# Branch products of two transformer layers: four-byte products replaced by three rounded products, with their high and low parts made beside the gates

## The reference, cut to what matters

```
gates = jax.nn.sigmoid(gate_logit)                 # u @ w_in, 4 * 1024 columns
branches = (y_pool, y_conv, y_moba, y_fox)
for n in range(N_BRANCH):
    term = gates[..., n * D_MODEL:(n + 1) * D_MODEL] * (branches[n] @ w_branch[n])
    merged = term if merged is None else merged + term
mixed = merged @ w_o
```

## Time and profile before

| | |
|---|---|
| median of 3 runs | 1328.84 us (1328.0 to 1331.78) |
| the profiled execution | 1324.11 us, of which the span is 1322.3 us |
| TensorE matmul busy | 1276.3 us, 97% of the span |
| VectorE busy | 933.9 us, 71% |
| ScalarE busy | 522.5 us, 40% |
| mean granted clock of TensorE | 0.996 |

### The profile page before, as it was taken

One profiled execution on the slowest core, in us unless ns is written; L12 is line 12 of the kernel. 1 busy time (PEld: TensorE's weight loads), 2 busy tenths in 40 slices (PEclk: granted clock), 3 DMA queues, 4 the chain that ended last, 5 costly groups with the idle time before them and its releaser, 6 DMA issues.

```text
span 1322.3 us, 18840 instructions
## 1 busy us (share of the span) xinstructions
PE 1276.3 (97%) x7793; PEld 1059.0 (80%) x7793; DVE 933.9 (71%) x1239; ACT 522.5 (40%) x805; POOL 107.9 (8%) x152
## 2 busy tenths in 40 slices
PE   5999999999999999999999999999999999999996
PEld 2798756448965479889988898987998998899895
DVE  5867687658768665777898666676587789654557
ACT  3322146214346043553344434334354434443432
POOL 2201110100000110011002000001011100000000
PEclk9999999999999999999999999999999999999999
DMA  9743550416620584677973776536567794355551
GB/s 372 243 139 106 180 188 1 150 45 237 206 80 1 187 273 155 241 281 272 314 276 131 252 250 249 191 128 255 187 238 264 276 332 170 127 190 182 184 185 56
DMA packets 104910, 257.75 MB, mean 195 GB/s; under 512 B 8213, under 2 KB 11766, under 8 KB 104570
## 3 DMA queue, kind: packets, MB, share of 16 engines
q1 hardware_dynamic: 80872, 172.40, 38.1%
q0 software_dynamic: 20192, 75.58, 15.9%
q10 hardware_dynamic: 3762, 8.57, 1.8%
HBM read 255.49 MB, written 1.05 MB: 194 GB/s over the span
## 4 chain that ended last, share of the span: by engine, by line
PE 82%; DVE 9%; ACT 4%; DMA 2%; issue 2%; POOL 1%; POOLq 0%; ACTq 0%; DVEq 0%
PE bank L823 80%; PE bank L990 3%; DVE weights_low L2327 1%; DMA start_ring<-in_w_mod_dram 1%; ACT odd_prob L1919 1%; DVE negated_maxima L2572 1%; DVE modulation_sums L2182 1%; ACT weights_high L1726 1%; ACT even_A L1860 1%; DMA even_yT<-in_w_mod_dram 1%; DVE even_A L2279 1%; DVE statistics L2294 0%; DVE x L2293 0%; DVE xn L2287 0%; DMA weight_ring<-in_w_in_dram 0%
## 5 line engine op out<-in xcount | busy, mean ns | idle before, releaser
L2327 DVE TENSOR_TENSOR weights_low<-weight_ring,weights_high 128x2048 fp32r<-128x2048 f32 (+1 forms) x120 | 261.8, 2184 | 202.0 <-ACT weights_high L1726 201.6
L1726 ACT ACTIVATE weights_high<-weight_ring 128x2048 fp32r<-128x2048 f32 (+1 forms) x120 | 219.7, 1831 | 316.2 <-PE bank L823 297.6
L823 PE MATMUL bank<-uT_high,weights_high 128*128 128x256 f32 (+1 forms) x1136 | 324.0, 285 | 0.2
L823 PE MATMUL bank<-uT_high,weights_low 128*128 128x256 f32 (+1 forms) x1136 | 321.3, 283 | 0.0
L823 PE MATMUL bank<-uT_low,weights_high 128*128 128x256 f32 (+1 forms) x1136 | 321.3, 283 | 0.0
L823 PEld LDWEIGHTS bank<-uT_high,weights_high 128*128 128x128 f32 (+1 forms) x1136 | 216.1, 190 | 2.9 <-issue 1.0
L823 PEld LDWEIGHTS bank<-uT_low,weights_high 128*128 128x128 f32 (+1 forms) x1136 | 216.2, 190 | 1.2
L823 PEld LDWEIGHTS bank<-uT_high,weights_low 128*128 128x128 f32 (+1 forms) x1136 | 216.2, 190 | 0.5
L2182 DVE SCALAR_TENSOR_TENSOR modulation_sums<-modulation_ring,silu_c_columns,modulation_sums 128x1024 f32<-128x1024 f32 x112 | 143.7, 1283 | 12.8 <-DMA modulation_ring<-in_w_mod_dram 5.4
L823 PE MATMUL bank<-weights_high,hidden_high 128*128 128x512 f32 x256 | 100.2, 391 | 0.2 <-DVE weights_low L2327 0.2
L823 PE MATMUL bank<-weights_low,hidden_high 128*128 128x512 f32 x256 | 99.8, 390 | 0.0
(11 more groups left out here) (337 smaller groups left out, 2195.5 us busy)
## 6 DMA issues: line engine op xcount, KB each, us to landing
weight_ring<-in_w_in_dram SPq DMA_DIRECT2D x52, 1024.0 KB, 5.8
modulation_ring<-in_w_ada_dram POOLq DMA_DIRECT2D x48, 1024.0 KB, 6.3
weight_ring<-in_w_down_dram SPq DMA_DIRECT2D x32, 1024.0 KB, 4.8
weight_ring<-in_w_up_dram SPq DMA_DIRECT2D x28, 1024.0 KB, 5.2
modulation_ring<-in_w_mod_dram POOLq DMA_DIRECT2D x16, 1024.0 KB, 5.6
weight_ring<-in_o_w_in_dram SPq DMA_DIRECT2D x10, 1024.0 KB, 5.0
norm_rows<-in_w_branch_dram SPq DMA_DIRECT2D x16, 512.0 KB, 5.8
weight_ring<-in_w_o_dram SPq DMA_DIRECT2D x8, 1024.0 KB, 7.9
```

Source lines behind the costliest of these rows:

```text
L823: return track(pe.matmul(*args, **kw))
L1726: act.activation(ring[:, s, c0:kn * cols], wring[:, slot, c0:kn * cols], ACT.Copy).then_inc(S["high_ready"], 1)
L2327: dve.tensor_tensor(lo[:, s, c0:kn * cols], wring[:, slot, c0:kn * cols], hi[:, s, c0:kn * cols].bitcast(F32), ALU.subtract).then_inc(w_fr ...
```

## The change

The product group becomes three rounded products as well. For each group g, ScalarE copies the branch weights to `branch_weights_high` (128 x 1024) right after the high part of the next gate's half 0 (`high_branch`), and VectorE makes `branch_weights_low` right after the low part of that half (`low_branch`), in the place of the raw weights. The rows of each branch are split too: branch 0's inside g = 0, the others' high parts at the start of g = 1, 3 and 5 and their low parts inside the same g (`high_rows`, `low_rows`; 128 x 512 each, the low part in the place of the rows). The high parts lie in buffers whose contents are no longer needed there. TensorE's product group now waits for `branch_low` and `rows_low`.

```
--- before.py
+++ after.py
@@ -236,6 +236,7 @@
     "high_ready": (len(FIRST_SPLIT), len(SPLIT_SLABS)), "u_ready": (KD, 12),
     "affine": (2, 4), "squares": (2, 4), "var_ready": (9, 4), "root_ready": (11, 8), "ctx_squares": (1, 0), "tile_out": (0, 0), "conv_ready": (0, 1), "merged": (0, 12), "sel_ready": (0, 1), "hdn_ready": (0, 8),
     "late_high": (0, 2), "late_low": (0, 3),
+    "branch_high": (0, 8), "branch_low": (0, 8), "rows_high": (0, 4), "rows_low": (0, 4),
 }
 
 
@@ -341,6 +342,10 @@
         wring = sb("weight_ring", [P, WSLOTS, WCOLS])
         mring = sb("modulation_ring", [P, 2, 4 * COLS])
         acc0 = sb("modulation_sums", [P, 2, D])
+        rounded_x = ExitStack()
+        sb("latent_rows_of_x", [P, TC, D], where=rounded_x)
+        ylow = sb("branch_rows_low", [P, 4, 2, N], F32R, where=rounded_x)
+        rounded_x.close()
         x = sb("x", [P, TALL, D])
         grow1 = sb("gate_row", [P, D])
 
@@ -452,6 +457,9 @@
 
 
         hyb = ExitStack()
+        rounded_xn = ExitStack()
+        bhigh = sb("branch_weights_high", [P, 2, 2, COLS], F32R, where=rounded_xn)
+        rounded_xn.close()
         xn = sb("xn", [P, TC, D], where=hyb)
         whigh = sb("weights_high", [P, SSLOTS, WCOLS], F32R, where=hyb)
         wlow = sb("weights_low", [P, SSLOTS, WCOLS], F32R, where=hyb)
@@ -459,6 +467,10 @@
         uhigh = sb("uT_high", [P, KD, N], F32R, where=hyb)
         ulow = sb("uT_low", [P, KD, N], F32R, where=hyb)
         merged = sb("mergedT", [P, KD, N], where=hyb)
+        rounded_rows = ExitStack()
+        blow = sb("branch_weights_low", [P, 2, 2, COLS], F32R, where=rounded_rows)
+        yhigh = sb("branch_rows_high", [P, 2, 2, N], F32R, where=rounded_rows)
+        rounded_rows.close()
         lnrow = sb("norm_rows", [P, 2, D], where=hyb)
         brow = sb("bias_rows", [P, 5, BW], where=hyb)
         lrow = sb("layer_rows", [R_N, P], where=hyb)
@@ -1502,19 +1514,16 @@
                     features_out(both(f"gate{j}"), [("gate", j, 0), ("gate", j, 1)], u, N, 2,
                                  wait=lambda k: between_halves(j, k))
                     n = j // 2
-                    pe.wait_ge(branch_full[j % 2], (4 * l + j // 2) * 16 + 16)
-                    w = branch_view(j)
-                    if n == 1:
-                        pe.wait_ge(S["conv_ready"], sec.at("conv_ready", 1))
-                    for job in ([("mixT",)], [], [("PV", 1)], [("PV", 3)])[n]:
-                        copied(job)
+                    pe.wait_ge(S["branch_low"], sec.at("branch_low", j + 1))
+                    pe.wait_ge(S["rows_low"], sec.at("rows_low", n + 1))
+                    w = [bhigh[:, j % 2, :, :], blow[:, j % 2, :, :]]
                     for i in range(2):
                         o = start(("prod", j, i))
                         for m in range(2):
                             for k in range(2):
-                                c = P * (2 * i + m)
-                                ins = product(o[:, N * m:N * m + N], w[:, k, c:c + P], yT[:, n, k, :],
-                                                start=(k == 0), stop=(k == 1))
+                                rows = [yhigh[:, n % 2, k, :], ylow[:, n, k, :]]
+                                ins = multiply(o[:, N * m:N * m + N], cut(w, k, P * (2 * i + m), P), rows,
+                                               start=(k == 0), stop=(k == 1))
                         done(ins, ("prod", j, i))
                     signal(ins, branch_free[j % 2])
 
@@ -2078,7 +2087,24 @@
                     act.wait_ge(late_in[h], l * 16 + 16)
                     act.activation(up_parts[h][0], up_raw[h], ACT.Copy).then_inc(S["late_high"], 1)
 
+                def high_branch(j):
+
+                    act.wait_ge(branch_full[j % 2], (4 * l + j // 2) * 16 + 16)
+                    act.activation(bhigh[:, j % 2, :, :], branch_view(j), ACT.Copy).then_inc(S["branch_high"], 1)
+
+                def high_rows(n):
+
+                    if n == 1:
+                        act.wait_ge(S["conv_ready"], sec.at("conv_ready", 1))
+                    for job in ([("mixT",)], [], [("PV", 0), ("PV", 1)], [("PV", 2), ("PV", 3)])[n]:
+                        copied(job)
+                    if n >= 2:
+                        act.wait_ge(branch_free[1], 4 * l + n - 1)
+                    act.activation(yhigh[:, n % 2, :, :], yT[:, n, :, :], ACT.Copy).then_inc(S["rows_high"], 1)
+
                 for g in range(8):
+                    if g in (1, 3, 5):
+                        high_rows((g + 1) // 2)
                     if g < 4:
                         for j in range(2):
                             o = ready(("S", g, j))
@@ -2090,10 +2116,14 @@
                             release(ins, ("S", g, j))
                     if g < 7:
                         high_part(f"gate{g + 1}", 0)
+                        high_branch(g)
+                        if g == 0:
+                            high_rows(0)
                         gate_tanh(g)
                         high_part(f"gate{g + 1}", 1)
                     else:
                         high_part("o0", 0)
+                        high_branch(7)
                         gate_tanh(7)
                         high_part("o0", 1)
                         for h in range(2):
@@ -2770,6 +2800,18 @@
                                           term[:, i, :].rearrange("p (m n) -> p m n", m=2), ALU.add
                                           ).then_inc(S["merged"], 1)
 
+                def low_branch(j):
+
+                    dve.wait_ge(S["branch_high"], sec.at("branch_high", j + 1))
+                    dve.tensor_tensor(blow[:, j % 2, :, :], branch_view(j), bhigh[:, j % 2, :, :].bitcast(F32),
+                                      ALU.subtract).then_inc(S["branch_low"], 1)
+
+                def low_rows(n):
+
+                    dve.wait_ge(S["rows_high"], sec.at("rows_high", n + 1))
+                    dve.tensor_tensor(ylow[:, n, :, :], yT[:, n, :, :], yhigh[:, n % 2, :, :].bitcast(F32),
+                                      ALU.subtract).then_inc(S["rows_low"], 1)
+
                 chunk = 2
                 for g in range(8):
                     if g < 4:
@@ -2794,9 +2836,15 @@
                         low(f"gate{g + 1}", 0)
                         if g == 4:
                             values_out(3)
+                        low_branch(g)
+                        if g == 0:
+                            low_rows(0)
                         low(f"gate{g + 1}", 1)
+                        if g in (1, 3, 5):
+                            low_rows((g + 1) // 2)
                     else:
                         low("o0", 0)
+                        low_branch(7)
                         copied(("gate", 7, 1))
                         for i in range(2):
                             dve.wait_ge(S["merged"], sec.at("merged", 8 + i + 1))
```

## The result

The changed kernel takes 1354.55 us (median of 4 runs, 1353.54 to 1356.68) against 1329.97 us (1328.0 to 1331.78) for the one before in the same comparison: a ratio of 1.0198, 95% interval [1.0173, 1.0222]. It is slower by 24.6 us where 23.6 were forecast. The profiled execution took 1356.68 us, its span is 1354.9 us and its mean granted clock 0.984 (before 0.996).

The account below looks back on a forecast made before the run. TensorE, busy for 97% of the span, was taken as the bound. Per layer 8.4 + 6.3 - 8 x 0.58 = +10.1 us, +11.8 with the clock; two layers +23.6, giving 1352.4 us, range 1341 to 1361.

Parts of the forecast that it names:

- The saving of TensorE: Product groups: eight products as 24 rounded instructions take 2.88 us instead of 3.46, saving 0.58 us a group, 9.3 in all.
- Group 0: Before product group 0 of each layer: TensorE waits 8.4 us for low parts behind VectorE's forget gate and slab.
- the sum: Whole kernel: +10.1 us a layer, +11.8 with the low clock, +23.6 us for two layers.
- Groups 1 to 7: Gate stage behind the first group: TensorE waits at g = 2, 3, 5, 6 and 7, 6.3 us a layer.
- The loop: Later groups: VectorE's way round, 16.25 us from gate end to next product group, exceeds TensorE's; a wait gives the next time.
- T(g): Gate stage: the moment at which TensorE has finished half 1 of gate g.
- S(g): Gate stage: the start of product group g, taken as equal to T(g) before the change.
- The clock: After the long wait in each layer: 3.4 us at 1.2 instead of 2.4 GHz delay the work by 1.7 us.
- A low clock that lasts longer, or comes after the short waits too: Rival, 12%, with rounded products no cheaper here as another case: each adds 3 to 8 us, about 1357 us.
- The cover: Rival, 3%: VectorE has low parts ready by T(g) in every group; only the 9.3 us saving remains, 1319.5 us.
- Only group 0 waits: Rival, 10%: the later groups have unseen slack and don't wait; +10.9 us remain, 1339.7 us.
- The clock doesn't fall: Rival, 15%: no low clock after the long wait; +20.2 us, 1349.0 us.

Follow-up runs that it names:

- e2_ahead: The changed kernel with branch weights split one group ahead from group 1 on, group 0 left alone: 1344.16 us, ratio 1.0109 to the kernel before.
- e1_group0: The changed kernel with branch 0's high and low parts made earlier, the low parts ahead of the forget gate: 1354.54 us, ratio 1.0195 to the kernel before.
- e4_busy: The changed kernel with 18 products of constants on TensorE ahead of its wait in group 0: 1354.94 us, ratio 1.0207 to the kernel before.
- e7_pay: The changed kernel with a one-column product carrying the slot-freeing signal ahead of the wait for low parts: 1355.57 us, ratio 1.0215 to the kernel before.
- r0_change: The changed kernel run again with no edit: 1356.88 us, ratio 1.0209 to the kernel before.

## Why the prediction was right

**The saving of TensorE.** Forecast 0.58 us a product group. In e2_ahead S(6) and S(7), with no wait between them, are 130.04 - 115.64 = 14.40 us apart, against 14.97 before: 0.57. This term held.

**Group 0.** Forecast 8.4 us, measured 8.22 of idle time (8.4 from start to start), in both layers, for the reason given: VectorE's forget gate and slab stand in front. The size held. Its meaning did not: the sum treats it as a term of its own, and e1_group0 shows that without it 1.2 us in front of gate 1 and 4.5 us at g = 1 come up, in stages of 140.95 and 143.23 us, where the change run again has 142.48 and 141.98. The expectation of e1_group0 made the same mistake, and was 20 us too low.

**Groups 1 to 7.** Waits in us; "after" is layer 1, where the clock was low only behind group 0, and e4_busy had no low clock in the stage:

| g | 1 | 2 | 3 | 4 | 5 | 6 | 7 | sum |
|---|---|---|---|---|---|---|---|---|
| forecast | 0 | 0.3 | 2.3 | 0 | 1.9 | 0.6 | 1.2 | 6.3 |
| after, layer 1 | 0 | 0 | 2.09 | 0.45 | 1.14 | 1.74 | 1.14 | 6.6 |
| e4_busy | 0 | 0 | 2.08 | 0.45 | 1.13 | 1.75 | 1.14 | 6.6 |
| e7_pay, layer 0 | 0 | 0 | 2.06 | 0 | 1.35 | 0.44 | 0.76 | 4.6 |

The loop is there, but the pattern isn't, and one step is the cause: "half 1 of the gate frees the slot for the next high part", which starts the loop at T(g). The release rides on the first instruction of the product group, so with a wait in front the loop starts at S(g). The rows from the changed kernel's group 6, S(6) = 669.79, first ScalarE's, then VectorE's:

```profile
670.27 1.91 ACT L1735 ACTIVATE weights_high<-weight_ring 128x2048 fp32r<-128x2048 f32 x1 [1.34 <-PE bank L835]
...
668.51 1.22 DVE L2806 TENSOR_TENSOR branch_weights_low<-norm_rows,branch_weights_high 128x1024 fp32r<-128x1024 f32 x1
672.21 2.29 DVE L2357 TENSOR_TENSOR weights_low<-weight_ring,weights_high 128x2048 fp32r<-128x2048 f32 x1 [2.48 <-ACT weights_high L1735]
674.42 1.28 DVE L2793 SCALAR_TENSOR_TENSOR branch_terms<-gate_tanh,bank 128x512 f32<-128x512 f32 x2
676.82 5.24 DVE L2212 SCALAR_TENSOR_TENSOR x<-modulation_ring,silu_c_columns,x 128x1024 f32<-128x1024 f32 x4
```

The second slab's low part starts at S(6) + 2.42. With 2.2 + 2.4 + 5.28 + 2.2 + 1.2 + 0.1 after that the period is 15.80 us, and 16.40 with a row part. The table of starts has just these for layer 1 from S(4) to S(7): 15.80, 16.40, 15.80. A wait no longer gives time to the next group; it is handed on whole. Before the change S(g) and T(g) were the same moment, and the trace couldn't tell them apart; the code of the owed signals could. With the signal paid before the wait (e7_pay) the alternation that was forecast comes back. Counted from start to start, which is how the forecast counts, S(1) to S(7) takes 103.36 us in e7_pay and 104.91 in e4_busy, against 100.29 before less 6 x 0.58 = 96.81. So the waits cost 6.5 us with the signal paid and 8.1 without, where 6.3 were forecast: the loop was read rightly for a signal that isn't held back, and the step was worth 1.6 us a layer. That the idle times of the table add up to 6.6, close to 6.3, is chance.

**The clock.** Priced at 1.7 us for each layer, from one stretch of 3.4 us. The mechanism held, the size was short. After group 0 the granted clock was low from 555.0 to 565.2 us in layer 0, of which TensorE worked from 559.06 on: 6.1 us at half speed, some 3.1 us lost. In layer 1 it was low from 995.3 to 1005.5, with work from 1000.64: 2.4 us lost. In r0_change, counted in the same way, 1.8 and 2.2 us were lost. And in layer 0 of the first profile it fell right after the wait of g = 3 (at 619.8) and after that of g = 6 (at 671.0) as well, for 3.4 us each, which costs up to 1.7 us each time. The windows around S(3) = 619.55:

```profile
618.00:620.00 2.00, 0.45 (x3) 0.45 (x4) 1.50 (x2) 0.44 (x2) 0.00 (x0) 0.95 0.32 22
620.00:622.00 2.00, 2.00 (x11) 2.00 (x11) 0.02 (x1) 1.91 (x1) 0.00 (x0) 0.50 0.93 348
622.00:624.00 2.00, 2.00 (x14) 2.00 (x13) 2.00 (x1) 0.00 (x0) 0.00 (x0) 0.69 0.40 155
```

A low clock that lasts longer, or comes after the short waits too, was a rival, at 12%, not the forecast.

**The sum.** Without the clock the forecast was +10.1 us a layer; e4_busy's stage has 140.04 - 128.34 = +11.7. Group 0 is 8.4 of that, and the saving of group 7 takes 0.6 off. S(0) to S(7) takes 122.47 us against 118.52 - 7 x 0.58 = 114.46: 8.0 us instead of 6.3. Of these, 6.6 are the idle times in the table. The rest lies mostly at the same places: a group that waited starts about 0.26 us later than its idle time alone says. Idle time is counted from the end at which the last matmul is shown, 0.16 us behind the moment at which a next one would have started, and the first product after a wait is shown 0.1 us longer. With the clock the stages grew by 13.6 to 16.6 us a layer where 11.8 were forecast. Two layers make 27.8 to 30.4 us, and the medians 24.6 and 28.6 in two comparisons. So the agreement to 1 us in the first comparison is partly luck: the stages had grown by more than was forecast, and the scatter of the runs took it back. The forecast was 1 to 5 us short by the medians, by the step named above and by the size of the clock term. Sign, place and range held.

**The rivals.** The cover did not hold (28.5 us of waits). "Only group 0 waits" fell with the waits from g = 3 on. "The clock doesn't fall" fell with the windows. The rounded products were as cheap as elsewhere.

## What to carry to other kernels

When a step is added to an engine with time to spare on average, look at the one place in its order where the waiting engine's work comes next: here the same 1.2 us steps made the stage some 7 us longer in one place than 2.2 us earlier, where no group behind group 0 had to wait. A wait that is seen may be only where a debt of several groups is paid, so follow the late engine's chain to its start before pricing its removal. And before placing a new wait, look for what rides on the instruction behind it, signals above all: they become late with it, and turn a single wait into one that every later round repeats.

## What the runs showed of the hardware

- The granted clock fell during the empty stretch of 8.22 us in front of group 0 and was low for 10.2 us in both layers of the changed kernel and in layer 1 of its repetition, for 6.8 us in the repetition's layer 0. In the changed kernel it was still at 0.50 in a window that started 3 us after TensorE had resumed.
- Waits of only 2 us in otherwise dense work were at times followed by low clock (0.50 at 620 to 622), at times not: layer 1 of the same execution had waits of 2.09 and 1.74 us without it. What decides it isn't shown.
- The first rounded product after a wait is shown 0.35 to 0.39 us long at full clock, where the others are shown 0.28 long.
- Near 150 us, long before the gate stages, the granted clock fell for 3 to 7 us in every profiled execution of this study but that of the kernel before. Some 2 us of the difference between the two profiles come from there. The change adds no instruction at that place; with one profile of the kernel before, whether the difference is chance is open.
